# Two kinds of attention in a fused fp32 network: the grid layer laid out by columns with 512 keys and two heads per step, and the windowed layers with two heads per step

## The reference

```python
start = clip(col - 8, 0, 64 - 16)
col_in = (col' >= start) & (col' < start + 16)      # keys that a query's column sees
s_loc = where(col_in, q @ k_grid * scale + rpb[row - row', col - col'], -inf)
s_ctx = q @ k_ctx * scale                           # 256 context keys, no bias
o = softmax(concat(s_loc, s_ctx)) @ concat(v_grid, v_ctx)
```

## Time and profile before

| what | value |
| --- | --- |
| three runs, us | 4327.49, 4331.46, 4334.54 (median 4331.46) |
| the profiled execution, us | 4335.81, its span 4334.0 |
| granted TensorE clock over the span | 0.952 of full speed |
| TensorE busy | 4029.7 us, 93% of the span |
| VectorE, ScalarE, GpSimd busy | 1845.5, 1441.6, 466.6 us |
| grid layer's units, first score to last value | 1321 to 1792 us |
| windowed units, first and second hybrid layer | 2457 to 2626 us, 3561 to 3708 us |

### The profile page before, as it was taken

One profiled execution on the slowest core, in us unless ns is written; L12 is line 12 of the kernel. 1 busy time (PEld: TensorE's weight loads), 2 busy tenths in 40 slices (PEclk: granted clock), 3 DMA queues, 4 the chain that ended last, 5 costly groups with the idle time before them and its releaser, 6 DMA issues.

```text
span 4334.0 us, 66723 instructions
## 1 busy us (share of the span) xinstructions
PE 4029.7 (93%) x28114; PEld 3570.8 (82%) x28114; DVE 1845.5 (43%) x3401; ACT 1441.6 (33%) x2876; POOL 466.6 (11%) x529
## 2 busy tenths in 40 slices
PE   6988899999989999899989989979997998997998
PEld 6866678888878777788878869979996886997998
DVE  3443454323334444544445444343335544434344
ACT  3444443212233333332322343333232224434322
POOL 1211120000012222100010000020002000002001
PEclk8988899999989999999999979989998998998999
DMA  4022112222331110133311102322321110222332
GB/s 165 25 88 83 52 39 72 98 98 98 98 107 44 35 34 28 40 103 101 103 53 40 49 18 69 91 63 89 93 83 44 40 45 23 77 91 65 93 93 74
DMA packets 86762, 303.75 MB, mean 70 GB/s; under 512 B 9392, under 2 KB 12592, under 8 KB 86336
## 3 DMA queue, kind: packets, MB, share of 16 engines
q1 hardware_dynamic: 84944, 292.72, 21.5%
q0 software_dynamic: 1520, 6.75, 0.5%
HBM read 297.34 MB, written 2.10 MB: 69 GB/s over the span
## 4 chain that ended last, share of the span: by engine, by line
PE 87%; ACT 5%; DVE 3%; POOL 2%; issue 2%; DMA 2%; ACTq 0%; SPq 0%; DVEq 0%; POOLq 0%
PE bank L472 58%; PE bank L534 6%; PE bank L954 3%; PE bank L825 2%; PE bank L503 2%; PE bank L803 2%; PE bank L943 2%; PE bank L740 1%; POOL scratch L2402 1%; PE bank L779 1%; PE bank L1046 1%; PE bank L624 1%; PE bank L813 1%; PE bank L1019 1%; PE bank L685 1%
## 5 line engine op out<-in xcount | busy, mean ns | idle before, releaser
L1688 DVE TENSOR_TENSOR weight_lo<-weight_raw,weight_hi 128x1024 fp32r<-128x1024 f32 (+1 forms) x464 | 561.5, 1214 | 564.3 <-ACT weight_hi L1123 564.1
L472 PE MATMUL bank<-u_hi,weight_hi 128*128 128x256 f32 (+1 forms) x2368 | 692.3, 292 | 8.0 <-DVE u_lo L2342 5.8
L472 PE MATMUL bank<-u_lo,weight_hi 128*128 128x256 f32 (+1 forms) x2368 | 678.4, 286 | 0.0
L472 PE MATMUL bank<-u_hi,weight_lo 128*128 128x256 f32 (+1 forms) x2368 | 677.6, 286 | 0.0
L1123 ACT ACTIVATE weight_hi<-weight_raw 128x1024 fp32r<-128x1024 f32 (+1 forms) x464 | 476.3, 1031 | 504.9 <-PE bank L472 370.6
L472 PE MATMUL bank<-h_hi,weight_hi 128*128 128x512 f32 (+1 forms) x1360 | 500.1, 368 | 24.2 <-DVE h_lo L2073 12.9
L472 PE MATMUL bank<-h_lo,weight_hi 128*128 128x512 f32 (+1 forms) x1360 | 478.4, 352 | 0.0
L472 PE MATMUL bank<-h_hi,weight_lo 128*128 128x512 f32 (+1 forms) x1360 | 478.0, 351 | 0.0
L472 PEld LDWEIGHTS bank<-u_hi,weight_hi 128*128 128x128 f32 x2368 | 454.8, 192 | 27.4 <-issue 17.6
L472 PEld LDWEIGHTS bank<-u_hi,weight_lo 128*128 128x128 f32 x2368 | 454.8, 192 | 0.0
L472 PEld LDWEIGHTS bank<-u_lo,weight_hi 128*128 128x128 f32 x2368 | 453.7, 192 | 0.1
(11 more groups left out here) (270 smaller groups left out, 7587.3 us busy)
## 6 DMA issues: line engine op xcount, KB each, us to landing
weight_raw<-in_w_mlp SPq DMA_DIRECT2D x128, 512.0 KB, 3.6
weight_raw<-in_w_ff SPq DMA_DIRECT2D x128, 512.0 KB, 3.6
weight_raw<-in_w_in SPq DMA_DIRECT2D x92, 512.0 KB, 3.6
weight_raw<-in_w_mod SPq DMA_DIRECT2D x80, 512.0 KB, 3.9
weight_raw<-in_a_w_qkv SPq DMA_DIRECT2D x24, 512.0 KB, 4.3
weight_raw<-in_b_w_qkv SPq DMA_DIRECT2D x24, 512.0 KB, 3.6
first_weight<-in_w_mod SPq DMA_DIRECT2D x16, 512.0 KB, 14.7
weight_raw<-in_w_ret_o SPq DMA_DIRECT2D x16, 512.0 KB, 3.6
```

Source lines behind the costliest of these rows:

```text
L472: m = e.matmul(view[:, 0:hi - lo], a[:, k, :], b[:, k0 + k, lo:hi], start=(k == 0 and i == 0), stop=(k == kt - 1 and i == 2))
L1688: e.tensor_tensor(wlo[s][:, 0:kt, :], raw[n % N_RAW][:, 0:kt, :], whi[s][:, 0:kt, :].bitcast(F32), ALU.subtract).then_inc(*tick("dve_split ...
```

## The change

The unit becomes a pair of heads with one query tile in both places: 8 units per group in the grid layer (32 pairs) and 20 and 16 pairs in the windowed layers. The number of fill calls halves and the total fill stays, so each call is twice as large.

- Grid layer: the host hands over the latents and the tables of the first two layers in column order (all 8 rows of a column together). A query tile is then 16 columns, and 32 columns (256 keys) hold everything it sees; with the 256 context keys it scores 512 keys instead of 768 (`near_keys`). For the two inner tiles the 256 keys come in pieces of 64 and 192, and the values that such a tile needs from half tiles are copied aside (`V_EDGE`).
- The scores of the two heads are issued alternately on the two halves of the partitions.
- The weights are divided by their sum before they are turned (`expo` on VectorE, 512 or up to 400 columns per head, in place of a division of 64 columns after the values).
- The values are the stationary operand now, 64 columns of one head at a time, and the turned weights move; the two heads write the lower and the upper half of the partitions of one bank. The result comes out with channels on partitions, so the turn at the end goes away.
- The bias tiles become 48 transfers of 256 columns with one pass each, into eight buffers.
- `to_rows`: GpSimd copies each of the eight blocks of the residual to row order and back, 16 copies of 128x512, after its part of the first group of the grid layer. The residual addition of that layer waits for it ("grid").

```diff
-        BAND = [sb(f"band{i}", [P, 14, 64], F32, o_lcl + i * 14 * 64 * 4) for i in range(2)]
...
+        BAND = [sb(f"band{i}", [P, 32, 8], F32, o_lcl + i * 256 * 4) for i in range(8)]
...
+        NS = [[ATTN[:, 512 * (2 * i + s):512 * (2 * i + s) + 512] for s in range(2)] for i in range(2)]
+        NWT = [ATTN[:, 2048 + 512 * s:2560 + 512 * s] for s in range(2)]
+        V_EDGE = [QK[i][:, 0:2, N_LAT:N_ALL] for i in range(2)]
...
-        WINDOW = [[(pr, qi, sub) for pr in range(4) for qi in range(5 - layer) for sub in range(2)]
...
+        NEAR = [(tt, qt) for tt in range(2) for qt in range(4)]
+        BANDS = [(g, tt, kind, sub) for g in range(4) for tt in range(2) for kind in range(3) for sub in range(2)]
...
+        def near_keys(qt):
+            ctx = (N_LAT, N_ALL)
+            if near_kind(qt) != 1:
+                return [(0, (0, 256)), (256, ctx)] if qt == 0 else [(0, (256, N_ALL))]
+            return [(0, (P * qt + P, P * qt + P + HD)), (HD, (P * qt - HD, P * qt + P)), (256, ctx)]
...
+        def near_values(b, qt):
+            local = [V[b][:, qt // 2 * 2 + i, :] for i in range(2)] if near_kind(qt) != 1 else \
+                [V_EDGE[b][:, qt - 1, :], V[b][:, qt, :]]
+            return local + [V[b][:, 4, :], V[b][:, 5, :]]
...
                 def score(i):
-                    tt, qt, sub = NEAR[i]
...
+                    views = [take("s", 1, g, i, s) for s in range(2)]
+                    pieces = near_keys(qt)
+                    for to, (a, c) in pieces:
+                        for s in range(2):
+                            r = slice(HD * s, HD * s + HD)
+                            m = e.matmul(views[s][:, to:to + c - a], QK[b][r, tt, P * qt:P * qt + P],
+                                         QK[b][r, 2 + tt, a:c], start=True, stop=True)
+                            if (a, c) == pieces[-1][1]:
+                                m.then_inc(*tick(("pe_scoreu", "pe_scorel")[s], ("s", 1, g, i, s)))
+                    for s in range(2):
...
                 def turn_weights(i):
-                    e.wait_ge(*at("w", 1, g, i))
...
+                    for s in range(2):
+                        view = take("t", 1, g, i, s)
+                        e.wait_ge(*at("n", 1, g, i, s))
+                        for k in range(4):
+                            m = e.transpose(view[:, P * k:P * k + P], NS[i % 2][s][:, P * k:P * k + P], ident)
+                        m.then_inc(*tick("pe_turn", ("t", 1, g, i, s)))
+                        close("t", 1, g, i, s)
...
                 def values(i):
-                    tt, qt, sub = NEAR[i]
...
+                    e.wait_ge(*at("wt", 1, g, i, 0))
+                    e.wait_ge(*at("wt", 1, g, i, 1))
...
+                    for k, v in enumerate(near_values(b, qt)):
+                        for s in range(2):
+                            v0 = P * tt + HD * s
+                            m = e.matmul(view[HD * s:HD * s + HD, 0:P], v[:, v0:v0 + HD], NWT[s][:, P * k:P * k + P],
+                                         start=(k == 0), stop=(k == 3))
...
-                def turn_out(i):
-                    tt, qt, sub = NEAR[i]
-                    if sub == 1:
-                        view = take("ot", 1, g, i)
-                        e.wait_ge(*at("out", 1, g, i))
...
+                    for s in range(2):
+                        view, x = take("t", 2, layer, i, s), WS[i % 2][s][0:nq]
+                        e.wait_ge(*at("n", 2, layer, i, s))
+                        for j in range(len(ts)):
+                            e.transpose(view[:, P * j:P * j + nq], x[:, 17 + P * j:17 + P * j + P], ident[0:nq, 0:nq])
+                        e.transpose(view[0:N_META, 384:384 + nq], x[:, 1:17], ident[0:nq, 0:nq]).then_inc(
+                            *tick("pe_turn", ("t", 2, layer, i, s)))
+                        close("t", 2, layer, i, s)
...
+                    keys = [(4, N_META, 384)] + [(j, P, P * n) for n, j in enumerate(ts)]
+                    for k, (j, nk, c) in enumerate(keys):
+                        for s in range(2):
+                            r = slice(HD * s, HD * s + HD)
+                            m = e.matmul(view[r, 0:nq], AV[0:nk, j, r], WWT[s][0:nk, c:c + nq], start=(k == 0),
...
+                    if layer == 1 and part < 2:
+                        r = (slice(HD, P), slice(0, HD))[part]
+                        e.activation(V_EDGE[b][r], tiles[r], ACT.Copy)
...
                 def expo(i):
-                    e.wait_ge(*at("max", 1, g, i))
...
+                    for s in range(2):
+                        x = NS[i % 2][s]
+                        e.wait_ge(*at("max", 1, g, i, s))
+                        e.activation(x, x, ACT.Exp, bias=small(i, s), accum_out=small(i, 2 + s)).then_inc(
+                            *tick("act_attn", ("w", 1, g, i, s)))
...
+                    e.wait_ge(*(at("o", 1, g, i - 1) if i else at("o", 1, g - 1, 7)))
+                    for s in range(2):
+                        job = ("t", 1, g, i, s)
...
+                        e.activation(NWT[s], view_of(*job), ACT.Copy).then_inc(
+                            *tick("act_attn", ("wt", 1, g, i, s), ("free", *job)))
...
                 def turn_out(i):
...
+                    e.wait_ge(*at("o", 1, g, i))
...
-                    tt, qt, sub = NEAR[i]
...
+                    for s in range(2):
+                        c = 48 * b + 8 * qt + 2 * tt + s
+                        sc, x, view = HQ[:, c:c + 1], NS[i % 2][s], view_of("s", 1, g, i, s)
+                        n = BANDS.index((g, tt, near_kind(qt), s))
+                        e.wait_ge(*at("band", n))
+                        e.wait_ge(*(at("t", 1, g, i - 2, s) if i > 1 else at("t", 1, g - 1, 6 + i, s)))
+                        e.wait_ge(*at("s", 1, g, i, s))
+                        e.scalar_tensor_tensor(out=x[:, 0:256], in0=view[:, 0:256], scalar=sc,
+                                               in1=BAND[n % 8][:, :, :].rearrange("p j r -> p (j r)"), op0=ALU.mult,
+                                               op1=ALU.add)
+                        e.tensor_scalar(x[:, 256:512], view[:, 256:512], sc, None, ALU.mult).then_inc(
+                            *tick("dve_attn", ("sc", 1, g, i, s), ("free", "s", 1, g, i, s)))
+                    for s in range(2):
+                        e.wait_ge(*at("sc", 1, g, i, s))
+                        e.tensor_reduce(small(i, s), NS[i % 2][s], AX, ALU.max, negate=True).then_inc(
+                            *tick("dve_attn", ("max", 1, g, i, s)))
...
+                def expo(i):
+                    for s in range(2):
+                        e.wait_ge(*at("w", 1, g, i, s))
+                    e.reciprocal(small(i, 4, 2), small(i, 2, 2)).then_inc(*tick("dve_attn", ("rc", 1, g, i)))
                     e.wait_ge(*at("rc", 1, g, i))
-                    e.wait_ge(*at("o", 1, g, i))
-                    e.wait_ge(*(at("ot", 1, g, 4 + qt) if tt else at("ot", 1, g - 1, 12 + qt)))
-                    e.tensor_scalar(OT[:, qt, N_LAT + HD * sub:N_LAT + HD * sub + HD], view_of("o", 1, g, i)[:, 0:HD],
-                                    small(i, 2), None, ALU.mult).then_inc(
-                        *tick("dve_attn", ("out", 1, g, i), ("free", "o", 1, g, i)))
-                sweep(len(NEAR), (score, nothing, nothing, values, nothing, nothing), fill)
+                    for s in range(2):
+                        x = NS[i % 2][s]
+                        e.tensor_scalar(x, x, small(i, 4 + s), None, ALU.mult).then_inc(
+                            *tick("dve_attn", ("n", 1, g, i, s)))
...
+                def bands(n):
+                    for s in range(2):
+                        before = BANDS[n + s - 8] if n + s >= 8 else None
+                        if before:
+                            e.wait_ge(*at("sc", 1, before[0], 4 * before[1] + (0, 2, 3)[before[2]], before[3]))
+                        h, kind = 4 * g + 2 * BANDS[n][1] + s, BANDS[n][2]
+                        if BANDS[n][0] > g:
+                            h += 4
+                        e.dma_start(BAND[(n + s) % 8][:, :, :].rearrange("p j r -> p (j r)"),
+                                    t["rpb"][3 * h + kind]).then_inc(*tick(f"dma_rpb{s}", ("rpb", n + s), by=16))
+                    for s in range(2):
+                        x = BAND[(n + s) % 8][:, :, :]
+                        e.wait_ge(*at("rpb", n + s))
+                        e.tensor_tensor(x, x, outside[kind].unsqueeze(2).to_broadcast([P, 32, 8]), ALU.add).then_inc(
+                            *tick("pool_attn", ("band", n + s)))
...
+                    if qt != 2 and n + 2 < len(BANDS):
+                        bands(n + 2)
...
+            def to_rows():
+                for k in range(KT):
+                    x, tmp = X[:, k, N_META:N_META + N_LAT], WT[:, 0:N_LAT]
+                    for span in range(2):
+                        e.wait_ge(*at("nt", ("n1", 1), k, span))
```

(5 more changed lines are left out.)

300 lines of the change are left out of this document (110 added, 190 removed).

## The result

The changed kernel takes 4079.39 us (median of four runs, 4076.10 to 4086.28), the kernel before 4333.02 us on the same chip (four runs, 4327.49 to 4337.46). The profiled execution took 4079.99 us, its span 4078.2.

What follows compares the result with a forecast made beforehand. TensorE, busy for 93% of the span, was taken as the bound. Grid work 133 us plus grid waits 12, less 2 for GpSimd, plus windowed layers 48 gave 191 us off 4331.5: 4140 us, range 4095 to 4210.

Steps and rivals of the forecast that it cites:

- Windowed layers: Windowed layers: 43 us of TensorE work saved, 51 at clock 0.85, and 3 us net of waits; 48 us entered the sum.
- More than forecast: Rival, chance 0.07: grid waits all vanish, grid clock goes to 1, windowed layers lose nothing; 4110 us.
- the chain of 4.2 us against 4.9 us of work: Windowed layers: ScalarE and VectorE round per pair against TensorE's work per pair, called close; 12 us lost.
- Grid layer, work: Grid layer, TensorE: scores save 60 us, transposes 16 and values 57, together 133 us.
- Grid layer, waits: Grid layer: 12 of the 19.5 us that values wait for ScalarE's copy go away.
- GpSimd: Grid layer: 16 copies at 1 us each delay bias tiles and low parts of weights; 2 us lost, range 0 to 12.
- The division: Grid layer: VectorE's division ahead of the transposes, 0.41 us per 512 columns, hidden by the projections.
- The halves don't overlap: Rival, chance 0.14: in the values a record costs 0.107 us, 24 us in grid and 25 in windowed layers; 4190 us.
- The windowed layers gain nothing: Rival, chance 0.13: the 4.2 us round with the sigmoids replaces what TensorE gives up there; 4188 us.
- TensorE at 1.2 GHz: Rival, chance 0.02: the granted clock falls as work between waits gets shorter, and the kernel ends slower; 4428 us.
- No change: Rival, chance 0.01: only if VectorE's bias wait recurred in every pair, 6 us x 32.
- The rule on a change of shape: Values blocks: changing tiling mode drains TensorE, at most 0.18 us per block, 12 us in all; sum changed little.

Runs made afterwards that it cites:

- e12: The changed kernel without GpSimd's 16 copies to row order, output not the reference's: 4073.31 us.
- e14: The changed kernel with GpSimd's eight steps to row order spread, one behind each unit of the second group: 4079.48 us.
- e6: The changed kernel with the windowed values issued one head after the other instead of in alternation: 4105.0 us.
- e7: The changed kernel with the grid layer's values issued one head after the other instead of in alternation: 4097.71 us.
- e1: The kernel before with the change in the windowed layers alone, grid layer untouched: 4236.84 us.
- e9: The changed kernel with three extra ScalarE copies ahead of each copy of turned weights in the windowed layers: 4245.97 us.
- e10: e3 with one extra ScalarE copy ahead of each copy of turned weights in the windowed layers: 4146.22 us.
- e5: The changed kernel with one extra ScalarE copy ahead of each copy of turned weights in the windowed layers: 4100.47 us.
- e13: The kernel before with windowed values as stationary operand per head, waits still per head, result not turned back: 4324.23 us.
- e3: The changed kernel with the turned weights as stationary operand again in the windowed values, without the turn back: 4103.46 us.
- e11: e10 with each head's values waiting for their own copy instead of one wait per pair: 4103.97 us.

## Why the prediction was wrong

**The step that failed** is the last paragraph of the change, "Windowed layers": "43 us at full clock, 51 us at the granted 0.85", then "9 us of 17.9" against "12 us lost, so 3 us net", 48 in all. The clock was taken as a property of the stretch and held fixed. It was an effect of the waits that the same paragraph halves. The earlier trace rows had the 48 us lost to it in sight (0.18 x 169 + 0.12 x 147); 37 to 45 came back (by the count, and at most), and no case of the prediction had them. Its rival "More than forecast" gave the windowed layers only the 12 us of waits and expected the clock to rise in the grid layer, where it stayed at 0.97.

**The second part of that step:** the chain of 4.2 us against 4.9 us of work, "close", was charged with 12 us lost. Measured, transposes and values wait 5.9 and 4.2 us in all, and idle fell by 25 us instead of growing by 3: the round through ScalarE and VectorE is hidden.

**The work there** was sized at 43 us at full clock and is 41 by the count, but this is luck: errors cancel. The values save 30 us where 39 were forecast. Of this, 7 us lie in the 0.061 us per record taken over from L722: a windowed block takes 1.17 and 0.95 us instead of 0.98 and 0.73, 0.2 us x 32 pairs. These blocks begin with the four short records of the meta keys, which L722 has not. The rest lies in the price before, 1.17 us per head in the earlier trace rows where 1.05 is the median. Against it, the turn at the end was worth 9 us instead of 4, and the transposes, put at nothing, gave 4. The 51 us "at the granted 0.85" belong to the failed step: they price the work at a clock that did not stay.

**Grid layer, work.** Forecast 133 us at full clock; TensorE is busy for 144 us less. The blocks after the change came out as worked: 1.12 + 0.79 + 1.02 = 2.93 us per pair against 2.86. The same count record by record gives 138 us at full clock: scores 60 (60 forecast), values 54 (57), transposes with the turn 22 (16), and the products between them 2. The term that was too small is the 0.10 us per transpose, read within a row of weight loads: six took 0.67 us on average and the turn 0.19. The remaining 6 us are clock. It stayed at 0.97, but over 153 us less: 0.03 x 471 against 0.03 x 318 is 5 us, which the sum left out.

**Grid layer, waits.** 12 us of 19.5 were taken away less 2 for GpSimd; idle fell from 25.4 to 16.8 us, 9 us. Right.

**GpSimd.** 16 copies were put at 1 us each; they take 1.11 and 0.62 us, 13.9 in all, and the 2 us lost are near the 3 us that the grid stretch gains in e12 and e14.

**The division** of 512 columns was put at 0.41 us from a row of 1040 columns and takes 0.53; the covers named for it held, with 6.9 us of wait at group starts.

**The rivals.** "The halves don't overlap" is refuted by the 1.02 us of L850 and priced by e6 and e7 at 26 + 18 = 44 us against the 49 worked out; a record by itself was put at 0.107 us and takes 0.095. "The windowed layers gain nothing" is refuted by e1. "TensorE at 1.2 GHz" had the wrong sign for this change, and its mechanism is real: e9 is what it looks like, up to 110 us of clock loss behind 72 us of added idle. It also put the windowed stretches at the lower level for "a sixth to a third"; a mean of 0.82 and 0.88 between levels of 0.5 and 1 is 36% and 24% of the time. "No change" is refuted.

**The rule on a change of shape.** In the row of the values, 0.33 us pass from the last product to the block instead of 0.23, and 0.34 us behind it instead of 0.23, 0.21 us for entering and leaving, against 0.08 behind the transposes, which change no shape. The Trainium skill, TensorEngine Tiling (Array Packing), Key Properties, states the drain without a price; the trace agrees, and its price is some 0.13 us per block here, 9 us for 68 pairs, near the 12 that I had as the most.

**On the clock.** The two levels and the return of the clock once waits were removed are in the rows above. The Trainium skill, TensorE: Matmul & The Clock Gate, HAM oscillation, describes a kernel that waits for data at every step and pays half of the time spent at the lower level. The trace agrees with the price, a little below it: at the lower level L534 starts every 0.21 us instead of 0.12, 1.8 times as long, and over the windowed units of the kernel before the count gives 40 us lost where half of the time at the lower level would be 47. It differs in the waits: those of the kernel before were 0.6 us on average and at most 0.8 for the copy, and at most 2.8 us elsewhere, far shorter than in that example.

**What stays open.** Removing the waits brought the clock back in every run. But the same added copy cost the clock 29 us with the old form (e10) and some 2 us with the new (e5), and the new form with the old rhythm (e13) kept 0.84 in one stretch and 0.94 in the other. Some joint effect of idle time and of what TensorE does between the waits is there; these runs don't name it.

## What to carry to other kernels

A granted clock below 1 in a stretch with many short waits can be time to be won, up to (1 - clock) x length, by a change that removes the waits, as in e3 and e11: give it a case of its own when you forecast, in both directions. Filling such waits with useless matmuls tells cheaply whether the waits hold the clock down; here it neither cost nor gained time that the runs can tell. Two heads on two halves of TensorE pay off in the values only if their matmuls alternate, and turning the operands for one head alone cost 0.11 us per head.

## What was not expected of the hardware

- Waits that leave TensorE busy for 87 to 89% of a stretch went with a clock of 0.82 and 0.88, and 418 records added in them brought it to 0.97 and 0.99 at no cost that the runs can tell (the two stretches were 11 us shorter in the profiled execution, the whole kernel 4 us by the ratio, with 0 within the interval).
- 85% busy with full clock exists too (e5), so the busy share does not decide alone.
- Column halves issued in series take 0.095 us per record of 128 columns, in alternation 0.064, in the grid layer; in the windowed one it is 0.14 against 0.07 with the short meta records among them. Row halves in series lose only 0.27 us of 1.18 and overlap anyway.
- A GpSimd copy of 128x512 takes 1.11 us where it writes with a stride and 0.62 us without.
